# A hybrid attention and expert layer on one core: small query pieces, split hand-over of a block's sums, sample rows doubled on chip, an early Gelu

## The reference, cut to what matters

```
x += W_out[concat(attention, conv)](rms_norm(x) @ W_in)
xb = rms_norm(x)
q  = (xb @ w_pq).reshape(t, 8 heads, 2, 128)
s  = einsum(q, sub_keys)                      # 2 x 128 scores per row and head
16 best of each half -> 256 sums -> 16 best sums -> 16 experts per row and head
g  = softmax(best sums)
h  = einsum('td,thkd->thk', xb, u_emb[expert])
x += einsum('thk,thkd->td', g * gelu(h), v_emb[expert])
y  = rms_norm(x) * g_final
```

## Time and profile before

| | |
|---|---|
| median of 3 runs | 3546.27 us |
| lowest and highest | 3508.42 and 3548.75 us |
| the profiled execution's own time | 3516.23 us |
| its span | 3514.5 us |
| expert stage, from its first dot to its last | 692.3 to 3496.5 us |
| DMA in the expert stage | share 0.95 to 1.01 in stretches of 100 us, about 415 GB/s |
| TensorE clock over the span | 0.857 of full speed |

### The profile page before, as it was taken

The page is one execution under the profiler, slowest core; times in us unless marked ns, Lnnn a source line. Parts: engine busy times, 40 slices in busy tenths (PEclk is TensorE's granted clock), DMA queues, the critical chain, the costliest instruction groups (busy, mean ns, idle before and its releaser), DMA issues. The chain is left out here.

```text
span 3514.5 us, 40801 instructions
## 1 busy us (share of the span) xinstructions
PE 2455.7 (70%) x13171; PEld 1007.7 (29%) x13171; DVE 2505.3 (71%) x6969; ACT 976.2 (28%) x2720; POOL 1389.1 (40%) x1203
## 2 busy tenths in 40 slices
PE   8999789675667666666766676667667666666755
PEld 4444456522222222222222222222222222222311
DVE  4888767677676777767777777677767767666875
ACT  3333344322222222222222222222222222222321
POOL 2333000144444445444444444444444444444443
PEclk9999889888888888988887898889877888888886
DMA  4000100699999999999999999999999999999997
GB/s 155 24 27 21 70 31 13 211 418 415 421 408 417 417 419 407 417 408 417 407 418 417 414 412 415 421 411 414 412 419 405 416 414 417 398 379 414 397 405 322
DMA packets 196573, 1198.91 MB, mean 341 GB/s; under 512 B 33108, under 2 KB 43368, under 8 KB 57121
## 3 DMA queue, kind: packets, MB, share of 16 engines
q0 software_dynamic: 156672, 1140.92, 79.1%
q1 hardware_dynamic: 39713, 55.65, 4.5%
HBM read 1181.66 MB, written 14.84 MB: 340 GB/s over the span
## 5 line engine op out<-in xcount | busy, mean ns | idle before, releaser
L1201 PE MATMUL ps<-uv_rows,diag 64*64 64x512 f32 x8704 | 1387.0, 764 | 960.5 <-ACT diag L1292 959.2
L1118 POOL DMA_INDIRECT uv_rows<-in_uv_emb,experts x1088 | 1262.5, 1160 | 1557.4 <-PE ps L1201 1328.5
L1434 DVE CUSTOM_DVE_ANT_0 uv_rows<-uv_rows,xn_c 128x1024 f32<-128x1024 f32 x1088 | 1334.3, 1226 | 758.6 <-DMA uv_rows<-in_uv_emb,experts 753.1
L1201 PEld LDWEIGHTS ps<-uv_rows,diag 64*64 64x64 f32 x8704 | 330.0, 156 | 1844.7 <-ACT diag L1292 1413.6
L1284 ACT ACTIVATE gelu_c<-dots 128x2 f32<-128x2 f32 x544 | 110.7, 204 | 1714.9 <-DVE dots L1434 1714.8
L1292 ACT ACTIVATE diag<-ident_twice,act_c 128x64 f32<-128x64 f32 x1088 | 319.2, 341 | 193.2 <-DVE act_c L1451 192.1
L522 DVE SCALAR_TENSOR_TENSOR convT<-w_out_sb,convT 128x128 f32 (+1 forms) x1080 | 276.3, 340 | 0.0
L1165 PE MATMUL ps<-w_pq_sb,xnT_c 128*128 128x256 f32 x1152 | 276.1, 394 | 0.0
L483 PE MATMUL ps<-w_in_sb,w_out_sb 128*128 128x512 f32 (+1 forms) x720 | 267.7, 527 | 11.3 <-ACT w_out_sb L391 11.3
L1165 PEld LDWEIGHTS ps<-w_pq_sb,xnT_c 128*128 128x128 f32 x1152 | 221.4, 197 | 104.5 <-issue 76.6
L483 PEld LDWEIGHTS ps<-w_in_sb,w_out_sb 128*128 128x128 f32 x720 | 124.6, 191 | 142.5 <-issue 125.1
(11 more groups left out here) (185 smaller groups left out, 2006.9 us busy)
## 6 DMA issues: line engine op xcount, KB each, us to landing
uv_rows<-in_uv_emb,experts POOLq DMA_INDIRECT x1088, 10.0
w_in_sb<-in_w_in SPq DMA_DIRECT2D x4, 2048.0 KB, 14.4
w_pq_sb<-in_w_pq SPq DMA_DIRECT2D x8, 1024.0 KB, 11.8
cat_turned<-catT SPq DMA_DIRECT2D x9, 512.0 KB, 2.6
w_out_sb<-in_x_prompt SPq DMA_DIRECT2D x8, 512.0 KB, 3.3
w_out_sb<-in_w_out SPq DMA_DIRECT2D x1, 4096.0 KB, 12.9
out<-x_c SPq DMA_DIRECT2D x8, 512.0 KB, 8.1
catT_c<-cat_turned SPq DMA_DIRECT2D x7, 512.0 KB, 8.2
```

Source lines behind the costliest of these rows:

```text
L1118: nc.gpsimd.indirect_dma_start(out=rows[:, m % RING, :], out_offset=None, in_=d.uv_emb[0], in_offset=bass.IndirectOffsetOnAxis(ap=experts[ ...
L1201: ins = pe.matmul(ps[dst, 2 * x + half, :], diag[src, (m + i) % DIAGS, :], rows[src, (m + i) % RING, cols], start=first, stop=last)
L1434: nc.vector.tensor_tensor_reduce(out=row, in0=row, in1=xn[:, block_of(n) % 2, :], scale=1.0, scalar=0.0, op0=ALU.mult, op1=ALU.add, accum_ ...
```

## The change

In phase B the convolution chain of the last block, the sample rows, runs two heads earlier (`conv_at`), and its `silu_exp` is issued in the loop. In phase C:

- `query` can be issued in parts, and the parts stand behind `weigh` at several steps. Turning, scoring and the copies move to later steps. In ACT's program the diagonals come before these copies. In heads with two routes the second one's score moves to the next head (`left_to`), and of the last routes one moves from head 64 to head 65.
- `crossed`, `add_residual` and the waits of the first `weigh` go by halves of 512 columns. In a boundary head `choose` pauses in the first steps. Several other steps move (turning the rows, adding the projection, normalising).
- The turned sample rows are loaded once, whole, and POOL copies one half over the other, in place of two loads of 64 columns.
- After each `gate_exps` ACT applies Gelu to one column (`back`).

```diff
+        def conv_at(b, head):
+            return head if b < s.NB else head - 2
...
-                if h == 7:
-                    hold(b)
...
+                if h == conv_at(b, 7):
+                    hold(b)
...
+            return {PROMPT - 2: [PROMPT + 1, PROMPT + 2], PROMPT - 1: [PROMPT + 3, PROMPT + 4], PROMPT: [PROMPT + 5],
+                    PROMPT + 1: [PROMPT + 6, PROMPT + 7]}.get(n, [])
...
-                    for half in HALVES:
-                        sp.dma_start(catT[:, :, half], d.catT[p][:, :, 0:s.TS]).then_inc(cat_here, 16)
+                sp.dma_start(catT[:, :, :], d.catT[p]).then_inc(cat_here, 16)
...
+                    if made_in(n, 0) == s.NB and k == K - 1:
+                        pool.wait_ge(cat_here, 16 * s.NB)
+                        nc.gpsimd.tensor_copy(catT[:, :, HALVES[1]], catT[:, :, HALVES[0]]).then_inc(cat_twice, 1)
...
-                if first and b >= 1:
-                    pe.wait_ge(sum_used, b)
-                    pe.wait_ge(crossed_out, b)
                 pe.wait_ge(diag_ready, m + 2)
-                for half in range(s.D // BANK):
+                for half in range(2):
+                    if first and b >= 1:
+                        pe.wait_ge(sum_used, 2 * (b - 1) + half + 1)
+                        pe.wait_ge(crossed_out, 2 * (b - 1) + half + 1)
...
-                if routed and n > 0:
-                    query(routed[0])
...
+                    if len(routed) == 1:
+                        if n > 0 and k in (1, 3, 5, 7):
+                            query(routed[0], k - 1, k + 1)
+                        if k == 9:
+                            turn_query(routed[0])
+                        if k == 11:
+                            score(routed[0])
...
+                if r > 0:
+                    act.wait_ge(gelu_back, r)
+                nc.scalar.activation(back[:, :], g.neg_half[:, :], ACT.Gelu).then_inc(gelu_back, 1)
...
+                    if n >= PH and n % PH == 0 and i == 0:
+                        crossed(n // PH - 1, 0)
                     gelus(n, i)
+                    if n >= PH and n % PH == 0 and i == 0:
+                        crossed(n // PH - 1, 1)
+                    diagonals(n, i)
...
                     if len(routed) == 1:
-                        if i == 0:
+                        if i == 4:
                             query_out(routed[0])
-                        if i == 2:
+                        if i == 5:
                             turned_out(routed[0])
-                        if i == 5:
+                        if i == 6:
                             scores_out(routed[0])
...
+                    if len(steps) == 1 and ends:
+                        for _ in range(0 if k < 4 or k == 5 else 1 if k < 12 else 2):
+                            next(steps[0], None)
...
+                    if ends and k == 1:
+                        add_residual(block_of(n) - 1, 0)
                     if k % GROUP == GROUP - 1:
                         weights(n, k // GROUP)
-                    if n >= PH and n % PH == 0 and k == 4:
+                    if ends and k == 1:
+                        add_residual(block_of(n) - 1, 1)
+                    if ends and k == 3:
                         add_crossed(block_of(n) - 1)
...
-                    if n >= PH and n % PH == 1 and k == 4:
+                    if n >= PH and n % PH == 1 and k == 9:
                         normalise(block_of(n) - 1)
```

More of the change, by code:

```diff
@@ L846, in _ @@
                     silu_exp(b - 1)
-            silu_exp(BLOCKS - 1)
+                if h == 6 and b == s.NB:
+                    silu_exp(b)
             outputs_out(BLOCKS - 1)
@@ L1010, in phase_c @@
         gf = sb("g_final_rows", [P, s.D])
+        back = sb("gelu_back", [P, 1])
         rms = sb("rms_c", [P, 3])
@@ L1041, in chosen_in, with left_to @@
                 return [n + 3]
-            first = PROMPT + 1 + 2 * (n - PROMPT + 2)
-            return [r for r in (first, first + 1) if r < LAST]
+            return {PROMPT - 2: [PROMPT + 1, PROMPT + 2], PROMPT - 1: [PROMPT + 3, PROMPT + 4], PROMPT: [PROMPT + 5],
+                    PROMPT + 1: [PROMPT + 6, PROMPT + 7]}.get(n, [])
         def routed_in(n):
             return chosen_in(n + 1)
+        def left_to(n):
+            return routed_in(n - 1)[1:] if n > 0 else []
         FIRST_ROUTED = 4
@@ L1155, in turn_rows, with query @@
                 ins.then_inc(xnT_psum, 1)
-            def query(r):
+            def query(r, lo=0, hi=s.DCH):
                 b, h = route(r)
[L1159 to L1164, removed]
+                if lo == 0:
+                    pe.wait_ge(xnT_ready, b + 1)
+                    if b == 0:
+                        pe.wait_ge(w_here[h], 16)
+                    if r > 0:
+                        pe.wait_ge(qT_out, r)
+                for x in range(lo, hi):
                     ins = pe.matmul(ps[:, Q_, 0:PAIR], xnT[:, x, :], w_pq[:, x, h * PAIR:(h + 1) * PAIR],
                                     start=(x == 0), stop=(x == s.DCH - 1))
-                ins.then_inc(q_psum, 1)
+                if hi == s.DCH:
+                    ins.then_inc(q_psum, 1)
             def turn_query(r):
@@ L1208, in project @@
                 if i == 0:
-                    pe.wait_ge(cat_here, 16 * p if p < s.NB else 16 * (p + 1))
+                    pe.wait_ge(cat_here, 16 * p)
+                    if p == s.NB:
+                        pe.wait_ge(cat_twice, 1)
                     pe.wait_ge(xnT_ready, p)
@@ L1235, in _ @@
                         project(made_in(n, 1), k)
-                    if made_in(n, 3) and k == 5:
+                    if made_in(n, 3) and k == 9:
                         turn_rows(made_in(n, 3))
[L1238 to L1251, removed]
+                    if left and k == 1:
+                        score(left[0])
+                    if len(routed) == 1:
[5 more added lines that the diff above has]
+                            score(routed[0])
+                    if len(routed) == 2:
+                        if k in (1, 3):
+                            query(routed[0], 2 * (k - 1), 2 * (k + 1))
+                        if k == 5:
+                            turn_query(routed[0])
+                        if k == 7:
+                            score(routed[0])
+                        if k in (9, 11):
+                            query(routed[1], 2 * (k - 9), 2 * (k - 7))
+                        if k == 13:
+                            turn_query(routed[1])
         @block.scalar
@@ L1292, in diagonals, with crossed @@
                     nc.scalar.mul(diag[:, m % DIAGS, :], ident_twice[:, :], act_w[:, n % 2, k:k + 1]).then_inc(diag_ready, 1)
-            def crossed(b):
+            def crossed(b, half):
                 act.wait_ge(weighed, K * PH * (b + 1) // 2 if b < s.NB else K * HEADS // 2)
+                cols = slice(half * BANK, (half + 1) * BANK)
                 for x in range(2):
-                    part = ps[HALVES[1 - x], 2 * x:2 * x + 2, :].rearrange("p a n -> p (a n)")
                     if b < s.NB:
-                        ins = nc.scalar.copy(xn[HALVES[x], b % 2, :], part)
+                        ins = nc.scalar.copy(xn[HALVES[x], b % 2, cols], ps[HALVES[1 - x], 2 * x + half, :])
                     else:
-                        ins = nc.scalar.copy(xn[HALVES[0], x, :], ps[HALVES[1], 2 * x:2 * x + 2, :].rearrange("p a n -> p (a n)"))
+                        ins = nc.scalar.copy(xn[HALVES[0], x, cols], ps[HALVES[1], 2 * x + half, :])
                 ins.then_inc(crossed_out, 1)
@@ L1351, in _ @@
                         gate_exps(chosen[-1])
-            crossed(s.NB)
+            for half in range(2):
+                crossed(s.NB, half)
         @block.vector
@@ L1538, in _ @@
                 inverse_gate(n)
+                ends = n >= PH and n % PH == 0
                 for k in range(K):
                     dot(n, k)
-                    if len(steps) == 1:
+                    if len(steps) == 1 and ends:
+                        for _ in range(0 if k < 4 or k == 5 else 1 if k < 12 else 2):
+                            next(steps[0], None)
+                    elif len(steps) == 1:
                         next(steps[0], None)
@@ L1572, in _ @@
                             pair_experts(v)
-            add_residual(s.NB)
+            for half in range(2):
+                add_residual(s.NB, half)
             add_crossed(s.NB)
```

73 lines of the change are left out of this document (34 added, 39 removed).

## The result

The changed kernel takes **3498.46 us** (median of 20 runs, 3494.45 to 3540.44); the kernel before took 3517.12 us beside it (20 runs). The ratio is **0.9938, 95% interval 0.9911 to 0.9966**: 18.7 us less, no change by the measure of 2%. The forecast was 3495.

The account below looks back on a forecast made before the run. Transfers were taken to bound the expert stage, at 39.75 us an undisturbed head. The terms summed to -35.3 us, put on 3529.9, the middle of two levels of known times, giving 3495 us; range 3458 to 3534.

Parts of the forecast that it names:

- Heads 3 to 7: 37 expert-stage heads: query in pieces and diagonals before the copies save two thirds of 23.7 us, -15.8.
- the hold-up: At a head's start, query products and copy delay the diagonals; buffers come free late, POOL issues no gather for 4.84 us.
- hidden after all: Rival: requests never ran short for long, transfers themselves are uneven; gain 0 to 20 us, about 3520; chance 0.22.
- Boundary heads: Seven heads: halves, earlier table load and pieces save two thirds of 11.8 us, -7.9.
- The early Gelu: One-column Gelus take the 1.28 us table load off the path at boundary heads, counted there; elsewhere nothing moves.
- Heads 61 to 66: Late heads: one route leaves head 64, saving about 3.0; parts and later scores save about 2.0; -5.0, bounds 0 and 12.4.
- Heads 1 and 2: 14 heads: normalising, store and load move later, transfers stay; a third of 12.1 us, -4.0.
- Phase B: End of phase B: the last store leaves earlier, at most 3.6 us; taken -3.0.
- Sample doubling: Sample rows loaded once and doubled by POOL's copy between two gathers; taken 0, without cover 2.6 us.
- The tail: Last rows: sums by halves put four copies and four sums on the path for two, +0.4 us.
- Head 57: Its 10.9 us begin with the sample residual's load, which stays; left alone, 0, bounds 0 and -10.9.
- Slower by TensorE's clock in heads 1: Rival: TensorE bounds heads 1; half speed in four of eight gives +97 us, about 3627; chance 0.05.

Follow-up runs that it names:

- e3_sample_split: Changed kernel with the sample residual rows loaded as two loads of 64 rows, not one with outer dimension 2; median 3490.38 us, ratio to before 0.9934.
- e9_dve_time: Changed kernel plus three unused 128x512 additions per head on DVE, adding DVE time with hardly any code; profiled 3498.3 us, heads 3 to 7 1493.3 us.

## Why the prediction was right or wrong

The number was right, 3.5 us off, but by luck: two errors cancel. The sum was -35.3 and the measured effect is -18.7, so 16.6 us of the gain did not come. The base, the middle of two levels (3529.9), was 12.8 us above the 3517.1 that before took in these runs.

- **Heads 3 to 7, -15.8: wrong**, measured -0.5 and -1.1. The step that failed is "two thirds" of 23.7 for the hold-up. The diagonals did come 2.5 us earlier, and head 20 with the dip of the earlier trace rows did lose 1.8 us that came back; but one head was taken for 37, and 25 of the 37 have no such dip. What the changed kernel has left in these heads is DVE's code: 25 heads with such a packet are 0.83 us longer than the other 12, and the rule gives 37 x 84 / 128 x 0.98 = 23.8. For the kernel before the same sum fits the 23.7 us, and its 24 heads with such a packet take 40.57 us, the other 13 take 40.05. There the dips and the code overlap; that the code's cost only showed in full once the dips were gone would be the rule of the larger cost again, and is an inference. The text's own test, "these heads stay as long with the hold-up gone", came out; this part is the rival "hidden after all", in its words "the transfers themselves are uneven". Heads 14 and 66, cited against taking it whole, fit it: head 14 has no packet of the second queue, and head 66, without a query, has its whole excess in one step of 3.99 us with a packet of PE's in it.
- **Boundary heads, -7.9:** right in size, measured -3.2 and -7.4, and 3.2 us from copies to `weigh` as forecast. The split was off: by one profile the early Gelu carries all of it, and that the halves bring nothing is no more than that profile shows.
- **The early Gelu:** its worth is at the boundaries, as the text said, 4 to 8 us, within the seven loads of 1.28 us (9.0 us) that were counted there. The drain of the Trainium skill (ScalarE: Activation LUTs, What ACT_TABLE_LOAD costs), up to 11 us more, does not show.
- **Heads 61 to 66, -5.0:** measured -3.9 and -7.1; head 64 took 41.16 us (-3.3, forecast -3.0).
- **Heads 1 and 2, -4.0:** measured -5.3 and -4.1.
- **Phase B, -3.0:** -2.2 by the rows above. **Sample doubling, 0:** nothing to see. **The tail, +0.4:** from the last dot to the end of the span it is 18.0 us before, 18.2 and 16.4 us after, so it can't be told.
- **Head 57, 0:** right, 94.4 and 94.6 us for heads 57 and 58; of its 10.9 us, e3_sample_split got 9.2 by another form of the load, so they could have been had.
- **Slower by TensorE's clock in heads 1:** did not come; these heads got shorter.

The two profiles lose 12.3 and 19.9 us from first to last dot; with phase B that is 14.5 and 22.1, around the 18.7 of the runs.

## What to carry to other kernels

Where the transfers are the bound and the DMA share is 1.0, look for a single DMA engine that is late: here packets of instructions, and a load with an outer dimension of 2, cost time at a share of 0.91 to 1.0, since a transfer over all 16 waits for the slowest. In an unrolled program count the instructions per engine. In these runs the engine whose code held its DMA engine longest set the pace, and time on the engine itself (e9_dve_time) did not matter. Before pricing a gap, look whether its excess is spread or sits in single steps of one size, and in how many of the heads the gap that you read really costs.

## What the runs showed of the hardware

- A block of some 128 instructions of DVE's costs about 0.98 us of one DMA engine (0.33, and 0.66 more on the row behind it), one of ACT's 0.71; 46 more DVE blocks cost 42 to 50 us, 28 more blocks of PE's nothing that shows. The Trainium skill (Runtime: NRT & Kernel Launch, Instruction fetch mechanics) calls the crossing of a block mostly hidden; where the DMA engines are full, these runs show that it is not.
- One POOL instruction of phase A (line 341, once line 339) lasts 31.0 to 31.6 us in five of the fourteen profiles, 0.2 to 0.4 us in the others. Why stays open, and so does whether the runs without a profile that are some 30 us longer have it too.
